# Weight conversions before attention steps, and three moved transposes, in a two-block float32 model on one core

## The reference

```
h = rmsnorm(x) * (1 + scale) + shift;  parts = split(h @ w_in)
y_a = mLSTM in both directions, normalised, times two gates      # 4 heads
y_b = (softmax(q1 k1) - lam * softmax(q2 k2)) v, normalised, gated  # 8 heads
y_c = real part of a 2-D Fourier transform, gated
y = g_a*(y_a @ w_a_out) + g_b*(y_b @ w_b_out) + g_c*(y_c @ w_c_out)
x = x + gate * (y @ w_out)
```

## Time and profile before

| what | value |
|---|---|
| time of the profiled execution | 2487.77 us |
| its span, first to last instruction | 2486.0 us |
| PE matmul busy | 2328.3 us (94%) |
| DVE busy | 1333.9 us (54%) |
| ACT busy | 1029.1 us (41%) |
| POOL busy | 248.4 us (10%) |
| mean granted clock of PE | 0.968 |

### The profile page before, as it was taken

The page is one execution under the profiler, slowest core; times in us unless marked ns, Lnnn a source line. Parts: engine busy times, 40 slices in busy tenths (PEclk is TensorE's granted clock), DMA queues, the critical chain, the costliest instruction groups (busy, mean ns, idle before and its releaser), DMA issues.

```text
span 2486.0 us, 38422 instructions
## 1 busy us (share of the span) xinstructions
PE 2328.3 (94%) x16176; PEld 2104.6 (85%) x16176; DVE 1333.9 (54%) x2731; ACT 1029.1 (41%) x1963; POOL 248.4 (10%) x252
## 2 busy tenths in 40 slices
PE   5999999999999999899999989998788999888998
PEld 3888878988878988699998889997578999767998
DVE  5544424576653223555556754467655555655554
ACT  2433312454432233444434453453544444544443
POOL 0100001312101121000022201201000100100110
PEclk7999999999999999899999999999989999988999
DMA  6321143211243212133332233463133544212543
GB/s 238 112 74 69 51 169 136 71 67 69 71 150 136 68 70 100 70 115 113 119 136 85 85 119 136 153 223 119 51 119 119 187 165 168 107 68 85 187 168 138
DMA packets 50412, 291.45 MB, mean 117 GB/s; under 512 B 8960, under 2 KB 13312, under 8 KB 19072
## 3 DMA queue, kind: packets, MB, share of 16 engines
q1 hardware_dynamic: 50240, 289.00, 32.4%
HBM read 286.89 MB, written 2.36 MB: 116 GB/s over the span
## 4 chain that ended last, share of the span: by engine, by line
PE 79%; DVE 13%; ACT 5%; issue 2%; DMA 1%; POOL 0%; DVEq 0%; SPq 0%; ACTq 0%; POOLq 0%
PE PS L503 76%; PE PS L507 2%; DVE wl L1915 2%; DVE wl L1917 2%; ACT TM L1343 1%; DVE TM L1896 1%; ACT wh L1353 1%; ACT TMG L1343 1%; DVE TM L1904 1%; DVE colS L1904 1%; DVE HYl L1904 1%; DVE colS L2382 1%; DVE TMG L1904 1%; DMA raw<-in_wpk 0%; DVE colS L2216 0%
## 5 line engine op out<-in xcount | busy, mean ns | idle before, releaser
L503 PE MATMUL PS<-HYh,wh 128*128 128x256 f32 (+1 forms) x3000 | 953.5, 318 | 43.4 <-DVE HYl L1904 22.4
L503 PE MATMUL PS<-HYl,wh 128*128 128x256 f32 (+1 forms) x3000 | 938.8, 313 | 0.0
L503 PE MATMUL PS<-HYh,wl 128*128 128x256 f32 (+1 forms) x3000 | 938.0, 313 | 0.0
L1915 DVE TENSOR_TENSOR wl<-raw,wh 128x1280 fp32r<-128x1280 f32 (+2 forms) x254 | 370.3, 1458 | 533.5 <-ACT wh L1353 533.4
L503 PEld LDWEIGHTS PS<-HYh,wh 128*128 128x128 f32 x3000 | 580.1, 193 | 85.2 <-DVE HYl L1904 24.2
L503 PEld LDWEIGHTS PS<-HYh,wl 128*128 128x128 f32 x3000 | 580.0, 193 | 30.5
L503 PEld LDWEIGHTS PS<-HYl,wh 128*128 128x128 f32 x3000 | 580.7, 194 | 29.1
L1353 ACT ACTIVATE wh<-raw 128x1280 fp32r<-128x1280 f32 (+2 forms) x254 | 306.9, 1208 | 357.0 <-PE PS L503 281.8
L503 PE MATMUL PS<-wh,HYh 128*128 128x256 f32 x1458 | 423.9, 291 | 10.7 <-ACT TM L1343 6.1
L503 PE MATMUL PS<-wl,HYh 128*128 128x256 f32 x1458 | 414.8, 285 | 0.0
L503 PE MATMUL PS<-wh,HYl 128*128 128x256 f32 x1458 | 414.8, 285 | 0.0
(11 more groups left out here) (180 smaller groups left out, 1780.4 us busy)
## 6 DMA issues: line engine op xcount, KB each, us to landing
raw<-in_wpk SPq DMA_DIRECT2D x235, 1024.0 KB, 4.8
raw<-in_wpk SPq DMA_DIRECT2D x32, 704.0 KB, 3.9
TM<-in_wpk SPq DMA_DIRECT2D x4, 1024.0 KB, 18.0
X<-in_xin SPq DMA_DIRECT2D x1, 2048.0 KB, 9.7
Y<-in_wpk SPq DMA_DIRECT2D x2, 1024.0 KB, 23.7
Y<-bias_d SPq DMA_DIRECT2D x4, 512.0 KB, 9.5
raw<-in_wpk SPq DMA_DIRECT2D x3, 512.0 KB, 3.5
T<-in_tabs SPq DMA_DIRECT2D x1, 1216.0 KB, 14.7
```

Of the source, the lines that this page charges most:

```text
L503: return P.x.matmul(o, l, r, start=start, stop=stop)
L1915: D.x.tensor_tensor(wl[:, s, 0:c], raw[:, r, 0:c], wh[:, s, 0:c], ALU.subtract).then_inc(*lo_split.mark())
```

## The change

It has five parts. **(A)** `b_out_slot`: in layer 1 the three output transposes of p = 0 to 2 stand one slot later, in 27, 39 and 51. **(B)** `merge` of branch a, layer 1: `last(3)` stands between gate 0 and gate 1 and not behind gate 1, on PE and ACT. **(C)** `merge` of branch c, both layers: the conversion stands ahead of `merged` 6 and 7 on ACT and DVE; before it stood behind 6 on ACT and behind both on DVE. **(D)** `slot_b` on DVE: the conversion stands directly behind `chunk_b`, and so ahead of `shares`, `B_DONE` and `B_OUT` of that slot. **(E)** `project_out` of layer 1 on DVE: the conversion stands ahead of `memory_low`.

```diff
@@ b_out_slot
-            return b_value_slot(l, p, 4 * g + 3) + ((8, 4), (2,))[l][g]
+            return b_value_slot(l, p, 4 * g + 3) + ((8, 4), (3,))[l][g]
@@ merge, on PE and in the same way on ACT
                     if j == 0:
                         gate(u, 0, 0)
-                        if l == 0 or br == "c":
-                            last(3)
+                        last(3)
                         gate(u, 128, 1, ("unit", u))
-                        if l and br == "a":
-                            last(3)
@@ merge, on ACT
                     if j == 7 and br == "c":
-                        merged(range(7))
+                        merged(range(6))
                     used("m_" + br, 8 * l + j)
                 if br == "c":
-                    merged((7,))
+                    merged((6, 7))
@@ merge, on DVE
-                    if br == "c" and j == 7:
-                        merged((6, 7))
                     used("m_" + br, 8 * l + j)
+                if br == "c":
+                    merged((6, 7))
@@ slot_b, on DVE
                 if chunk is not None:
                     chunk_b(l, chunk)
+                if unit:
+                    used(*unit)
                 if pj and b_turn_slot(l, *pj) == n + 1:
                     shares(*pj)
...
-                if unit:
-                    used(*unit)
@@ project_out, on DVE
-                        if l == 1:
-                            memory_low(0, k)
                         if h and (l or j < 3):
                             used("w_out", 4 * l + j)
                         if l == 1:
+                            memory_low(0, k)
                             if k:
```

## The result

| | median us | lowest to highest | executions |
|---|---|---|---|
| before | 2487.66 | 2481.33 to 2488.49 | 4 |
| changed | 2502.39 | 2501.05 to 2503.36 | 4 |

The ratio is 1.0068, with a 95% interval of 1.0056 to 1.0081: 14 to 20 us slower, where +8.7 was forecast. It is taken over all executions, 21 of the changed kernel with a median of 2503.36 us; the table has four of each, and their medians lie 14.7 apart. The profiled execution of the changed kernel took 2503.75 us (span 2502.0), 16.0 more than that of before.

What follows compares the result with a forecast made beforehand. PE, busy for 94% of the span, was taken as the bound. Terms -8.9 + 2.9 + 2.0 + 8.1 + 0.4 = +4.5, plus +4.2 for half clock, gave +8.7: 2496.5 us, range 2490 to 2503.

Steps and rivals of the forecast that it cites:

- part A's term of -8.9: Layer 1 output transposes: three waits vanish (-5.7 us) and two half-clock stretches with them (-3.2).
- The prediction's own sign of being wrong: PE's standing time not growing by 4 to 5 us, or a wait over 3 us at an unnamed place.
- B: Layer 1, merge of branch a: PE waits 2.9 us for a_hn at the four transposes now ahead of gate 1.
- C: End of merge of branch c: chunks 6 and 7 come later, +0.5 us in layer 0 and +1.5 in layer 1.
- D in branch b: Layer 0 projections: DVE reaches the next scores' maximum later; PE's 0.57 us wait becomes 2.0, twice: +2.9.
- D in merge_b: Layer 0, slots 64 to 72: shares and a low output wait for the conversion, +5.2 us in sum.
- D in layer 1: Shares at the head of a slot and outputs in odd slots, so no cost: 0.
- E: Layer 1 project_out: +1.9 us at chunk 7, against a vanishing 1.50 us wait for wl: +0.4.
- Half clock: Behind some half of the long new PE waits: 2.6 half-clock stretches at 1.6 us each, +4.2 us.
- The -3.2 in A: Layer 1: two 3.40 us stretches at clock 0.53 behind the first two output waits vanish, 1.6 us each.
- Standing time: Whole kernel: PE's total standing time grows by 4 to 5 us against before.
- Rival 3: Layer 1 output transposes bring nothing, as output is late or they hold up the next scores: 2505.4 us, chance 0.06.

Runs made afterwards that it cites:

- d_late: Kernel before plus the conversion moved ahead in slot_b, with output transposes later (layer 0: slots 42, 58; layer 1: 32, 44, 51): 2486.74 against 2486.16 us.
- D alone: Kernel before with only the conversion moved ahead in slot_b on DVE: 2502.03 against 2486.54 us, ratio 1.0066.
- c_only: Kernel before with only the conversion moved ahead of merged 6 and 7 in merge of branch c: 2490.77 against 2486.16 us, ratio 1.0012.
- b_only: Kernel before with only last(3) moved between gate 0 and gate 1 in layer 1: 2488.07 against 2486.16 us, ratio 1.0001.
- a_order: Kernel before with layer 1's output transposes one slot later and, on DVE, the previous slot's conversion put behind the low output: 2479.82 against 2485.65 us.
- a_only: Kernel before with only layer 1's three output transposes one slot later: 2489.83 against 2486.54 us, ratio 1.0018.
- a_late: Kernel before with layer 1's output transposes in slots 32 and 44 for p = 0 and 1, and one slot later for p = 2: 2478.27 us, ratio 0.9972.
- all_late: The whole change, but with the output transposes at the places of d_late: 2491.86 against 2486.16 us, ratio 1.0023.

## Why the prediction was wrong

The direction and most of the terms held, and the size did not. The step that failed is part A's term of -8.9. The three waits did go, but the prediction put nothing in their place, by the sentence "No DVE or ACT work of that slot is queued behind a conversion, since odd slots have none". In their place stand two waits, of 3.74 and 3.75 us, with half clock behind them. Two things were missed:

1. I asked when the operand of the transposes is ready (it is; they don't wait), but not who waits for their **result's place**. The transposes fill bank 6, and the next key product needs it.
2. DVE runs a slot behind PE. The conversion of slot 26 stands in no odd slot, but it does stand between the transposes of slot 27 and DVE's read of them.

For A and D together in layer 1 the prediction had -8.9 + 0; the changed kernel has +2.5, an error of 11.4. All other terms together were +17.6 with the clock term, and the ledger has 17.2. The agreement in sum is partly luck. The untouched stretches took 3.6 off, which no term foresaw, and that hid part of the error. The prediction's own sign of being wrong showed: waits of more than 3 us at a place that it didn't name. By terms:

- **B** +2.9: the wait is 2.85. The ledger's +3.9 in the changed kernel has a part at half clock in it.
- **C** +2.0: +3.1 by the ledger; layer 0 came out as 0.90 for 0.5, and layer 1 as +1.9 for +1.5.
- **D in branch b** +2.9: +4.3, by another mechanism, the same bank. The forecast wait (2.0 at 548) is real, 1.68 in `d_late`, but the bank's wait covers it in the changed kernel. In slot 20 it is not the instruction of POOL that begins 1 us into the piece that comes first: one of 1.29 us was running since 474.58, before the piece began at 475.01.
- **D in merge_b** +5.2: +5.2, with waits of 1.20, 1.83 and 1.43 for 1.4, 2.0 and 1.6.
- **D in layer 1** 0: wrong by itself, where it is +5.3. In the changed kernel A's and D's wait at the key product are one wait: A alone +2.8, D alone +5.3, both +2.5.
- **E** +0.4: +0.7 by the ledger; the wait of 1.50 vanished as said.
- **Half clock** +4.2 for "some half of the long" waits: the stretches came, but behind others than I had listed. In the changed kernel the key product's waits have it in both layers, and the waits of merge_b (1.20 to 1.83) and C (2.53) have full clock. But it doesn't belong to the place: C's wait has 0.72 behind it in `c_only`, B's has 1.00 in `b_only`. Which term the 4.2 should have been can't be told from these runs. The -3.2 in A rests on a reading that is slightly off too: the stretch behind the second wait, at 1404.90, has 0.64 and not 0.53.
- **Standing time**: the "4 to 5 us" of the last paragraph is a sum with half clock in it. Without the -3.2 the terms give +7.7, and 12.2 was measured.
- **Conversions brought forward** are three parts (C, D, E) and not "four of the five". The sum doesn't use it.

Rival 3 (A brings nothing) was the case that came nearest in time (2505.4), and I gave it 0.06. Its mechanism was wrong too: the output was not late. That the bank explains the waits is shown by `a_order`, which against `a_only` changes DVE's order alone, and by `a_late` and `all_late`, which change the places alone.

## What to carry to other kernels

When a write to PSUM is moved later, look for who takes that bank next and what stands on the reading engine between the write and the last read; the wait shows up on an instruction that never touches the data, with the reader's output named in its bracket. Count the reading engine's lag: "this slot" on DVE may be the next one on PE. And cost the parts of a change in pairs: two edits that delay the same read (A and D here) don't add.

## What the hardware showed that was not expected

- Beside POOL's work DVE's instructions with two SBUF inputs grow: the second conversion piece from 0.95 to 1.48 and, in `a_order`, 2.05; the first from 1.49 to 2.04 and 2.20; the softmax weights from 0.75 to 1.23. The low output, which reads PSUM, stays at 0.74. POOL's instructions grow as well: the one of 128x512 takes 1.27 at 1376.91 of the changed kernel, where DVE's instruction beside it has one input, and 2.42 at 1361.74 in `a_order`. The Trainium skill ("SBUF — State Buffer", "SBUF: two separate sides") has the later of the two blocked for the whole instruction. The rows of `a_order` agree: POOL's 2.42 begins while the first piece runs, to 1363.01, and ends 1.15 after that; the second piece begins at 1362.93, POOL's ends at 1364.16, and the piece 0.82 after that. The growth depends on how much of the other instruction is left: the 1.48 is a growth of 0.53.
- One and the same wait had different clocks behind it in different runs: B's 2.85 us 0.72 in the changed kernel and 1.00 in `b_only`, C's 2.53 us 1.00 in the changed kernel and 0.72 in `c_only`, and the wait of 2.00 us for the second output, which neither B nor C touches, 0.64 before and 1.00 in `b_only` (from 1403.90). Waits of 1.82 in branch b had 0.65 and 0.54. The length of a wait alone doesn't tell whether half clock follows; what does stays open.
